# Who multiplies the masked C·B block by the forward step sizes in the Mamba-2 SSD steps

## The reference, cut to what matters

```
seg = cum[:, :, None, :] - cum[:, None, :, :]
decay = jnp.exp(jnp.where(lower[None, :, :, None], seg, -jnp.inf))
xdt = xc * dtc[..., None]
scores = jnp.einsum('blhn,bshn->blsh', cc, bc) * decay
y = jnp.einsum('blsh,bshp->blhp', scores, xdt)
```

## Time and profile before

| | us |
|---|---|
| median of 3 runs (1841.21 to 1842.01) | 1841.83 |
| the profiled execution's own time | 1834.07 |
| its span, first to last instruction | 1832.8 |
| PE busy | 1567.7 (86%) |
| DVE busy | 1170.1 (64%) |
| ACT busy | 730.9 (40%) |
| POOL busy | 401.7 (22%) |
| POOL L912, the product, 48 instructions | 70.0 (1473 ns each) |
| mean granted PE clock, as a share of full speed | 0.901 |

### The profile page before, as it was taken

How to read it: one execution, slowest core, us unless ns; L and a number is a source line. 1 busy time by engine, 2 the same in 40 slices (tenths; PEclk the granted TensorE clock), 3 DMA queues, 4 the chain that set the end, 5 groups by cost and what they waited for, 6 DMA issues and landing times.

```text
span 1832.8 us, 22605 instructions
## 1 busy us (share of the span) xinstructions
PE 1567.7 (86%) x8489; PEld 1280.4 (70%) x8489; DVE 1170.1 (64%) x1672; ACT 730.9 (40%) x1291; POOL 401.7 (22%) x405
## 2 busy tenths in 40 slices
PE   5699898888976968988879699998996889998876
PEld 2577786667765858766547577776785778887755
DVE  0258877888767275455556733635439588988876
ACT  1435444444433242355553322322324354554442
POOL 0013343343442034100000600000006023332331
PEclk7589999999978988999999799989997899999888
DMA  9332445424441303322431343453321234333332
GB/s 286 119 95 77 125 121 161 137 83 148 115 138 46 115 25 95 92 77 64 137 116 46 104 140 99 130 161 110 120 87 35 74 116 115 92 109 99 100 108 92
DMA packets 169276, 197.38 MB, mean 108 GB/s; under 512 B 9680, under 2 KB 151632, under 8 KB 169168
## 3 DMA queue, kind: packets, MB, share of 16 engines
q1 hardware_dynamic: 158336, 163.08, 28.3%
q0 software_dynamic: 9296, 30.19, 6.5%
q10 hardware_dynamic: 1536, 2.67, 0.4%
HBM read 194.59 MB, written 1.31 MB: 107 GB/s over the span
## 4 chain that ended last, share of the span: by engine, by line
PE 54%; DVE 28%; issue 8%; ACT 7%; DMA 2%; ACTq 0%; POOL 0%; DVEq 0%; POOLq 0%
PE ps L342 14%; PE ps L343 14%; PE ps L344 14%; DVE xc L745 7%; DVE w_lo L325 5%; DVE cum_b L753 3%; PE ps L365 2%; ACT w_hi L319 2%; PE ps L498 2%; PE ps L504 2%; DMA raw<-in_mod_w 1%; DVE h_lo L1267 1%; PE ps L1507 1%; DVE cum_b L755 1%; PE ps L1523 1%
## 5 line engine op out<-in xcount | busy, mean ns | idle before, releaser
L342 PE MATMUL ps<-h_hi,w_hi 128*128 128x512 f32 (+1 forms) x1088 | 425.2, 391 | 24.5 <-DVE w_lo L325 12.8
L343 PE MATMUL ps<-h_lo,w_hi 128*128 128x512 f32 (+1 forms) x1088 | 410.3, 377 | 0.0
L344 PE MATMUL ps<-h_hi,w_lo 128*128 128x512 f32 (+1 forms) x1088 | 410.2, 377 | 0.0
L325 DVE TENSOR_TENSOR w_lo<-raw,w_hi 128x1024 fp32r<-128x1024 f32 (+1 forms) x214 | 285.8, 1368 | 173.7 <-ACT w_hi L319 172.2
L319 ACT ACTIVATE w_hi<-raw 128x1024 fp32r<-128x1024 f32 (+1 forms) x214 | 216.7, 1047 | 151.4 <-PE ps L344 126.6
L342 PEld LDWEIGHTS ps<-h_hi,w_hi 128*128 128x128 f32 x1088 | 210.8, 194 | 73.2 <-issue 36.5
L344 PEld LDWEIGHTS ps<-h_hi,w_lo 128*128 128x128 f32 x1088 | 209.5, 193 | 37.8
L343 PEld LDWEIGHTS ps<-h_lo,w_hi 128*128 128x128 f32 x1088 | 210.7, 194 | 35.2
L342 PE MATMUL ps<-w_hi,h_hi 128*128 128x512 f32 (+2 forms) x448 | 161.6, 361 | 39.8 <-DVE h_lo L1267 18.6
L745 DVE SCALAR_TENSOR_TENSOR xc<-ps,gp,xc 128x508 f32<-128x508 f32 (+1 forms) x224 | 162.4, 727 | 47.5 <-ACT xc L619 41.3
L343 PE MATMUL ps<-w_lo,h_hi 128*128 128x512 f32 (+2 forms) x448 | 157.7, 352 | 0.0
(11 more groups left out here) (222 smaller groups left out, 2675.8 us busy)
## 6 DMA issues: line engine op xcount, KB each, us to landing
raw<-in_mod_w SPq DMA_DIRECT2D x96, 512.0 KB, 4.7
raw<-in_ssm_w_in SPq DMA_DIRECT2D x64, 512.0 KB, 5.5
cum_b<-cum_scratch POOLq DMA_DIRECT2D x96, 256.0 KB, 5.4
raw<-in_ssm_w_in SPq DMA_DIRECT2D x66, 256.0 KB, 4.1
raw<-in_ssm_w_out SPq DMA_DIRECT2D x32, 512.0 KB, 4.0
raw<-in_pool_w_in SPq DMA_DIRECT2D x32, 512.0 KB, 4.4
raw<-in_attn_w_in SPq DMA_DIRECT2D x20, 512.0 KB, 3.7
raw<-in_pool_w_out SPq DMA_DIRECT2D x16, 512.0 KB, 4.0
```

What stands on the lines that cost most here:

```text
L325: dve.tensor_tensor(w_lo[:, n % WS, 0:width], raw[:, r % RS, 0:width], w_hi[:, n % WS, 0:width].bitcast(F32), ALU.subtract).then_inc(lo_do ...
L342: pe.matmul(o, hi_s, hi_m, start=first, stop=False)
L343: pe.matmul(o, hi_s, lo_m, start=False, stop=False)
L344: return pe.matmul(o, lo_s, hi_m, start=False, stop=last)
```

## The change

GpSimd's `forward_part` goes away. The same product becomes the first instruction of each mix(n) on VectorE, and writes the same buffer of `Wa`. L772 then waits for it on the same engine. The waits on `wa_g` are gone; the masks wait for `w_d` instead, before they overwrite `cb`. The product of chunk n waits for the L775 of two chunks before (`m_d`, one back), and for `cbdt_a`, which stood before L772 already.

```diff
         def masks():
             dve.wait_ge(s["t1_p"], 4 * g + 4)
             if g:
-                dve.wait_ge(s["wa_g"], nc * g)
+                T["w_d"].wait(dve)
                 dve.wait_ge(s["cbdt_a"], nc * g)
...
         def mix(n):
             c = first + n
+            if nc * g + n >= 2:
+                T["m_d"].wait(dve, 1)
             dve.wait_ge(s["cbdt_a"], nc * g + n + 1)
-            dve.wait_ge(s["wa_g"], nc * g + n + 1)
+            T["w_d"].inc(dve.tensor_tensor(Wa[:, n % 2, :, :], cb[:, 0, c, :].unsqueeze(1).broadcast_to((128, HG, 128)),
+                                           by_head(sg[:, g, 32 + 4 * c:36 + 4 * c], (128, HG, 128)), ALU.mult))
+            T["w_d"].wait(dve)
             T["w_d"].inc(dve.tensor_tensor(Wb[:, n % 2, :, :], Wb[:, n % 2, :, :], Wa[:, n % 2, :, :], ALU.add))
...
-        def forward_part(n):
-            c = first + n
-            pool.wait_ge(s["cbm_d"], 2 * g + 1)
-            if nc * g + n >= 2:
-                pool.wait_ge(s["w_d"], nc * g + n - 1)
-            pool.tensor_tensor(Wa[:, n % 2, :, :], cb[:, 0, c, :].unsqueeze(1).broadcast_to((128, HG, 128)),
-                               spread(sg[:, g, 32 + 4 * c:36 + 4 * c], 128), ALU.mult).then_inc(s["wa_g"], 1)
-
...
-        forward_part(0)
-        forward_part(1)
...
-        for n in range(2, nc):
-            forward_part(n)
```

## The result

| | median, us | runs | profiled execution | its span | granted clock |
|---|---|---|---|---|---|
| before | 1841.52 | 4 (1837.01 to 1842.01) | 1834.07 | 1832.8 | 0.901 |
| after | 1857.83 | 4 (1856.61 to 1859.3) | 1859.3 | 1858.1 | 0.901 |

Ratio 1.0094 [1.0076, 1.0113]: slower by 16.3 us, where +18.2 and 1860.0 were forecast. I therefore compare the traces by steps and take the total from the medians.

The account below looks back on a forecast made before the run. PE and DVE hand the end to each other, neither saturated. Direct parts 2.3 + 2.2 + 4.9 = +9.4 us, clock 8.0 + 0.8, together +18.2: 1841.83 to 1860.0 us, range 1848 to 1869.

Parts of the forecast that it names:

- Removed: decay(0) stalls beside POOL vanish; relief on the path, capped by ACT's first tap: 0.98 us in layer 0, 0.72 layer 3.
- rival 2: POOL's y takes the lock before L755 in decay(0), so taps(1) gains nothing: 10.2 us more, 1870.2; chance 0.1.
- Added: Each mix gets one 512-column product on VectorE with a dependent instruction behind: 0.72 us, 1.44 a pair of mixes.
- rival 3: New instructions dearer or more on the path: all 48 give 34.6 us, 1876.4, with the clock 1884; chance 0.07.
- rival 5: ACT's cap is absent and the new instruction costs 0.60 us, relief and cost meet: about 1843; chance 0.08.
- Layer 0: Direct part: steps 2 to 6 +0.46 us each, +2.3; steps 1, 7 and 8 together +2.2.
- PE's clock: Layer 0: idle before the latent scan grows from 0.66 to 2.10 us; falls in 7 of 10 steps at 2.3, +8.0.
- Rival 1: PE's clock does not fall in layer 0 despite the longer idle before the latent scan: 1851.2 us; chance 0.2.
- Rival 4: Layer 0's idle before the first modulation sum shortens 0.98 us, the clock no longer falls: faster, 1835.2; chance 0.05.
- Layer 3: Step 1 +1.4 us, steps 2 to 7 +4.3, step 8 -0.8, together +4.9; clock in step 1 another +0.8.
- step 8: Layer 3's last step: POOL's last two products take 2.03 us from DVE, against 1.44 added; taken as -0.8.
- Between trace and median: The profiled execution lies 7.8 us below the runs' median and this carries over: 1852.3 profiled, 1860.0 median.

## Why the prediction was right

The mechanism was the forecast's, the sum was 18.2 for 16.3. By its steps:

- **Removed.** A relief of 0.98 a step was forecast, capped by ACT's first tap; 0.96 was measured (21.25 to 20.29) and 0.97 with the stall alone taken away. (The lines quoted for it give 378.16 - 377.15 = 1.01; the 0.03 us between ACT's end and taps(1) was taken off without a word.) In layer 3 the way from the masks to the first state went from 15.87 to 15.16 in the steps 2 to 6, 0.71 for the 0.72 forecast. After the change y came second, 0.44 us behind L755, so rival 2 falls. The rule named in the prediction, the Trainium skill (SBUF — State Buffer, section Who interferes with whom), also says that a VectorE instruction with no more than one SBUF input, outside the engine's two-port modes, doesn't contend with GpSimd. The single wait bears it out: the gates keep their 1.28 us beside POOL's products.
- **Added.** 0.72 from product to dependent addition was taken, 0.71 to 0.72 measured. mix(0) and mix(1) stayed hidden, with 2.15 us of idle left before L386; rival 3 falls (the 22 us of lost relief that it names are in neither of its two times). Removing and adding did not cancel on the path, so rival 5 falls too.
- **Layer 0.** 2.3 + 2.2 was the direct part. With PE's idle filled a step is 0.8 us longer than in the first trace of before, where 0.46 was forecast; neither of the two traces has a fall behind the scan. That is 1.5 us too little over five steps.
- **PE's clock.** The idle before the scan was put at 2.10 and measured at 2.12. The forecast was a fall in 7 of 10 steps at 2.3 us, +8.0; it fell in 5 of 5 at 2.4 us by the steps, and the filling gave 9.8 back. Rival 1 falls by that. Two readings under this term were weaker than they look. "After 0.66 us it never fell" holds for that one trace; over nine traces it fell in 17 of 45. And of the six idles in layer 3 only five are of 2.44 us, that of step 7 is 8.20. The nearness of 2.10 to 2.44 was the argument, and it held. Rival 4 falls by 4.70 us of idle (forecast 4.67) before the first modulation sum: the clock still fell behind it.
- **Layer 3** holds the mis-sized term, step 8. Forecast were +4.9 and +0.8. In the steps 1 to 7 the traces show +6.0 where 6.5 were forecast (1.4, 4.3 and 0.8), so that part was right. Step 8 was put at -0.8, from 2.03 us of POOL's products against 1.44; the traces give -2.7 in the mean, and layer 3 timed alone +1.8 [1.1, 5.0] instead of +5.7. Layer 0 gave 14.9 instead of 12.5 (4.5 and 8.0). The two misses have opposite signs; that the total came out closer than its parts is luck.
- **Between trace and median.** I carried the 7.8 us between profile and median over to the changed kernel. It did not hold: the profiled executions of after lie at its median or 1.5 above. The forecast by medians was unharmed. Why the first trace of before is so much faster than its median is not shown; that it has no fall behind a latent scan, where the second has one, could be a part of it.

## What to carry to other kernels

Work moved to an engine costs what its place costs: the same 48 instructions cost 16 us as moved, and nothing once the half of layer 0's that stood behind VectorE's wait for PE was made inside it. Before you move work because two engines block each other, try a wait that puts it beside instructions that don't clash; here one wait on POOL took the whole relief of decay(0) in both layers and none of the cost, -6.8 us. And count what a longer wait of PE does to its clock: it was up to 9.8 of the 16 us lost here, and throw-away matmuls in the waits were worth 18 us. Look at the clock in more than one trace of the kernel before, too.

## What the runs showed of the hardware that was not expected

- 2.12 us of idle ahead of the scan, 16 matmuls of 64 columns, was followed by a fall to half speed in 20 of 20 steps of four traces. After 0.66 us in the same place it fell in 17 of 45 steps of nine traces, later and more briefly, and not always in the same steps of the same kernel (none in the first trace of before, one in the second).
- PE's own work can be cheaper with more of it: 40 extra matmuls took 9.8 us off the changed kernel.
- ACT's order, one function call moved, took 11.6 us off, partly by VectorE's idle that went, partly by fewer falls of PE's clock. The two were not told apart.
- POOL's two products of 128x512 took 3.02 us beside decay(0) and 2.04 beside the gates.
